# Two attention loops on one core: the logits of two pairs ahead are issued behind the transposes of the current pair

## The reference

```python
# first layer, per block of 128 queries; k_sel, v_sel are the selected keys and values
logits = jnp.einsum('bqgrd,bqkgd->bqgrk', qg, k_sel).astype(jnp.float32) * (ATT_HEAD_DIM ** -0.5)
logits = jnp.where(valid[:, :, None, None, :], logits, -jnp.inf)
p = jax.nn.softmax(logits, axis=-1).astype(dt)
o = jnp.einsum('bqgrk,bqkgd->bqgrd', p, v_sel)
# third layer, block-causal mask
s = (jnp.einsum('bqhd,bkhd->bhqk', qn_b, k_nope)
     + jnp.einsum('bqhr,bkr->bhqk', qp_b, k_pe)).astype(jnp.float32) * scale
s = jnp.where(mask[None, None], s, -jnp.inf)
p = jax.nn.softmax(s, axis=-1).astype(v.dtype)
o = jnp.einsum('bhqk,bkhd->bqhd', p, v)
```

## Time and profile before

| | us |
|---|---|
| runs, median of 3 | 1187.79 |
| runs, lowest and highest | 1187.22, 1194.19 |
| the profiled execution, its own time | 1192.98 |
| its span in the trace | 1190.9 |
| PE busy | 1102.4 (93%) |
| PE weight loads busy | 959.4 (81%) |
| DVE busy | 461.9 (39%) |
| ACT busy | 553.6 (46%) |
| POOL busy | 818.3 (69%) |
| mean granted clock of PE | 0.972 of full |

### The profile page before, as it was taken

How to read it: one execution, slowest core, us unless ns; L and a number is a source line. 1 busy time by engine, 2 the same in 40 slices (tenths; PEclk the granted TensorE clock), 3 DMA queues, 4 the chain that set the end, 5 groups by cost and what they waited for, 6 DMA issues and landing times.

```text
span 1190.9 us, 15744 instructions
## 1 busy us (share of the span) xinstructions
PE 1102.4 (93%) x6630; PEld 959.4 (81%) x6630; DVE 461.9 (39%) x825; ACT 553.6 (46%) x745; POOL 818.3 (69%) x297
## 2 busy tenths in 40 slices
PE   7989999999999655999999989999887998999997
PEld 7877788888899644778888879999886896788886
DVE  4673311159508899531110051711255535111102
ACT  5682544443455564354444344455633534544430
POOL 5703699789498566359979839796575273898880
PEclk9999999999999876999999999999998999999999
DMA  8203655554565300275555435554344144755540
GB/s 347 102 7 120 234 177 179 192 192 146 177 227 191 112 1 1 108 252 189 177 182 189 159 141 213 177 177 147 122 154 143 37 142 159 243 181 178 182 170 36
DMA packets 27445, 186.45 MB, mean 157 GB/s; under 512 B 3168, under 2 KB 3424, under 8 KB 5872
## 3 DMA queue, kind: packets, MB, share of 16 engines
q1 hardware_dynamic: 25184, 178.83, 43.2%
q10 hardware_dynamic: 2192, 6.62, 1.8%
HBM read 184.39 MB, written 1.05 MB: 156 GB/s over the span
## 4 chain that ended last, share of the span: by engine, by line
PE 81%; DVE 12%; POOL 3%; ACT 3%; issue 1%; DMA 1%; DVEq 0%; SPq 0%; ACTq 0%
PE ps L369 25%; PE ps L371 24%; PE ps L370 24%; POOL wl L353 3%; DVE arena L1545 2%; DVE arena L1546 1%; PE ps L1209 1%; PE ps L1939 1%; ACT wh L349 1%; DVE arena L1560 1%; DMA stage<-in_tiles 1%; PE ps L1074 1%; DVE arena L836 1%; DVE arena L814 1%; DVE arena L1554 1%
## 5 line engine op out<-in xcount | busy, mean ns | idle before, releaser
L353 POOL TENSOR_TENSOR wl<-stage,wh 128x2048 fp32r<-128x2048 f32 x166 | 764.6, 4630 | 295.8 <-ACT wh L349 263.9
L349 ACT ACTIVATE wh<-stage 128x2048 fp32r<-128x2048 f32 (+1 forms) x168 | 318.5, 1906 | 89.7 <-DMA stage<-in_tiles 89.1
L369 PE MATMUL ps<-wh,xh 128*128 128x512 f32 (+2 forms) x776 | 293.4, 378 | 20.3 <-POOL wl L353 7.0
L371 PE MATMUL ps<-wh,xl 128*128 128x512 f32 (+2 forms) x776 | 287.9, 371 | 0.0
L370 PE MATMUL ps<-wl,xh 128*128 128x512 f32 (+2 forms) x776 | 287.5, 370 | 0.0
L369 PE MATMUL ps<-xh,wh 128*128 128x256 f32 x644 | 184.1, 286 | 8.5 <-DVE xl L2009 4.1
L369 PEld LDWEIGHTS ps<-wh,xh 128*128 128x128 f32 x776 | 146.8, 189 | 49.7 <-POOL wl L353 5.7
L370 PE MATMUL ps<-xl,wh 128*128 128x256 f32 x644 | 182.7, 284 | 0.0
L371 PE MATMUL ps<-xh,wl 128*128 128x256 f32 x644 | 182.7, 284 | 0.0
L371 PEld LDWEIGHTS ps<-wh,xl 128*128 128x128 f32 x776 | 146.6, 189 | 25.6
L370 PEld LDWEIGHTS ps<-wl,xh 128*128 128x128 f32 x776 | 146.9, 189 | 24.1 <-issue 0.5
(11 more groups left out here) (347 smaller groups left out, 1130.3 us busy)
## 6 DMA issues: line engine op xcount, KB each, us to landing
stage<-in_tiles SPq DMA_DIRECT2D x167, 1024.0 KB, 4.9
arena<-in_ln_g ACTq DMA_DIRECT2D x4, 512.0 KB, 3.5
arena<-in_ln_b ACTq DMA_DIRECT2D x4, 512.0 KB, 5.1
arena<-in_x_t SPq DMA_DIRECT2D x1, 1024.0 KB, 5.3
x_res<-in_x SPq DMA_DIRECT2D x1, 1024.0 KB, 20.5
out<-x_res SPq DMA_DIRECT2D x4, 256.0 KB, 2.2
stage<-in_tiles SPq DMA_DIRECT2D x1, 544.0 KB, 7.4
arena<-in_pre_mix_norm ACTq DMA_DIRECT2D x1, 512.0 KB, 7.0
```

What stands on the lines that cost most here:

```text
L349: nc.scalar.activation(wh[:, ring(n), part], stage[:, ring(n), part], ACT.Copy).then_inc(hi_done, 1)
L353: nc.gpsimd.tensor_tensor(wl[:, ring(n), :], stage[:, ring(n), :], wh[:, ring(n), :].bitcast(F32), ALU.subtract).then_inc(lo_done, 1)
L369: mm(out_, lh, rh, start=start, stop=False, skip_group_check=skip)
L371: return mm(out_, ll, rh, start=False, stop=stop, skip_group_check=skip)
```

## The change

In attend_pe, the block that waits for lg_free and issues logits(i + 2) moves from ahead of the wait for pn_ready(i) to behind the transposes of pair i. PE's turn is then transposes(i), logits(i + 2), value(i - 1). Both attention loops use the function. ACT's and DVE's lists stay as they are, and no buffer or size changes.

```diff
             for i in range(2):
                 logits(i).then_inc(lg_ps.sem, lg_ps.up())
             for i in range(pairs):
-                if i + 2 < pairs:
-                    pe.wait_ge(lg_free.sem, lg_free.due(pe))
-                    logits(i + 2).then_inc(lg_ps.sem, lg_ps.up())
                 pe.wait_ge(pn_ready.sem, pn_ready.due(pe))
                 if i >= 1:
 
...
                         last = nc.tensor.transpose(ps[:, 4 + e, c * P:(c + 1) * P],
                                                    lg[i % 3][:, e, c * P:(c + 1) * P], ident[:])
                 last.then_inc(pt_ps.sem, pt_ps.up())
+                if i + 2 < pairs:
+                    pe.wait_ge(lg_free.sem, lg_free.due(pe))
+                    logits(i + 2).then_inc(lg_ps.sem, lg_ps.up())
                 if i >= 1:
                     value(i - 1)
```

## The result

| | before, us | changed, us |
|---|---|---|
| median | 1190.99 (4 runs) | 1222.54 (4 runs) |
| lowest, highest | 1187.22, 1197.57 | 1220.60, 1224.74 |
| profiled execution, its span | 1190.9 | 1218.6 |
| first loop: first L814 to the first product behind the loop | 32.76 | 54.10 |
| second loop, measured the same way | 23.06 | 34.06 |

The ratio is 1.0259, with a 95% interval of 1.0203 to 1.0315: slower. The two medians differ by 31.6 us. In the two profiled executions the loops lost 21.3 and 11.0 us, and 4.65 us came back between them, in a stretch whose program the change does not touch (last experiments). "First product behind the loop" is the matmul at L369 that starts the next block of weight products.

The account below looks back on a forecast made before the run. DVE was taken to bound the first loop and PE's logits the second. The loops' added 19.0 + 11.6 = 30.6 us, from serial waits and half clock, gave 1218.4 us from a median of 1187.79; range 1208 to 1226.

Parts of the forecast that it names:

- What bounds the loops: Before the change, DVE paces the first loop at 3.57 us a pair; in the second DVE waits for PE's logits.
- The ring: Both loops: normalised(i), transposes(i), logits(i + 2), masked(i + 2), normalised(i + 1) run serially; 5.80 and 8.44 us, adding 13.4 and 8.4.
- transposes until the next group's weight loads: Ring term on PE in both loops: time from the transposes' start to the logits' weight loads, 0.80 us.
- The clock: PE's pauses in both loops halve its granted clock, adding 2 x 1.29 + 2 x 1.5 and 2 x 1.6 us.
- I count two of the four at 1.5 each: First loop's four further pairs, with 2.3 us of PE pause: two assumed at half clock, 1.5 us each.
- the tail: End of the first loop, pairs 6 and 7, with no logits left to issue: forecast unchanged.
- One to one behind the loops: Behind the loops: all work is tied to their end, so their delay passes on whole, none absorbed.
- That the clock stays up: Rival, both loops: the pauses leave PE's clock up, giving 1209.6 us; chance 0.19.
- That every pair falls: Rival, both loops: every pair falls to half clock, giving 1224.0 us; chance 0.24.
- PE did not take the logits past the waiting transposes: Denies a rival on PE's order: logits taken while transposes wait, leaving 1187.8 us; chance 0.02.
- the other side: Rival, not slower: second loop's transposes no longer stand behind logits, saving 0.8 us, giving 1187.0 us; chance 0.01.
- The sum by long pauses alone: Both loops' added time if only the four PE pauses longer than 2.90 us halve the clock: 27.6 us, or 1215.4.

Follow-up runs that it names:

- last experiments: Kernel before and changed kernel, each with an added POOL wait that keeps its L353 off DVE's L2037 and L2039; 1187.96 and 1220.37 us.
- e3: Changed kernel's order within a turn, but with logits issued three pairs ahead instead of two; 1194.15 us, ratio 1.0002 to the kernel before.
- e9: Changed kernel plus a POOL wait until DVE has rotated the queries ahead of the second loop; 1220.37 us, ratio 1.022 to the kernel before.
- e10: Changed kernel with e9's POOL wait and unused matmuls filling PE's pauses in both loops; 1207.89 us, ratio 1.0117 to the kernel before.
- e1: Kernel before with the new order in the first attention loop only; 1215.12 us, ratio 1.016.
- e2: Kernel before with the new order in the second attention loop only; 1209.38 us, ratio 1.011.
- e7: Kernel before plus a POOL wait until DVE has rotated the queries ahead of the second loop; 1186.99 us, ratio 0.9944.
- e8: Kernel before, unchanged, run once more; 1194.92 us in one run.
- e12: Kernel before with e7's POOL wait, run again on the chip of e9 and e10; 1187.96 us, ratio 0.9939 to the kernel before.

## Why the prediction was right

The forecast was 1218.4 us in a range of 1208 to 1226, from a difference of 30.6 us on a median of 1187.8. The measured median is 1222.5, the difference 31.6, with the median of before at 1191.0 once a further run joined it. That the two differences agree within 1 us is partly luck: the ratio's interval leaves 24 to 38 us. The loops themselves lost 32.3 us in the profiles.

- **What bounds the loops** held: DVE sets the pace of the first, PE of the second.
- **The ring** held, and e3 shows it is the mechanism: the same order without the ring costs nothing. Its length was 5.61 us, not 5.80, and 8.23, not 8.44. The term too large was "transposes until the next group's weight loads", 0.80, taken from a row in which values follow transposes. With logits behind them the loads come 0.60 to 0.61 us after the transposes start (85.10 - 84.50 in e3). So the first ring came to 12.3 us instead of 13.4, the second to 30.77 - 23.06 = 7.7 instead of 8.4.
- **The clock** was too small for the first loop: 5.6 us forecast, 9.05 measured (54.10 - 45.05). The step that erred is "I count two of the four at 1.5 each": pairs 2, 3 and 4 all ran slow, with 7.17, 7.27 and 7.07 us a pair against 5.61, pair 5 did not (5.62). The first two long pauses cost 1.05 and 1.92, not 1.29 twice, and the tail, which the forecast left unchanged, lost the remaining 1.4 (clock 0.52 from 112.0 to 115.3 us; transposes(7) lasted 1.40 us). In the second loop 3.2 was forecast and 34.05 - 30.77 = 3.3 measured, though not as forecast: one ring was slow by 1.67 us (9.90 against 8.23), the other kept its 8.23, and the rest fell behind them.
- **The errors cancelled in part:** the rings 1.8 us less, the clock 3.5 more. This, too, is luck.
- **One to one behind the loops** held: e9 shows 32.4 us of the 32.8. The profiled executions alone would have hidden this, as they differ by 27.7: the missing 4.65 us are the collision, there in the profile of before and not in that of the changed kernel, and no part of the forecast. It is also why transposes(2) of the second loop started at 964.87 and not near 969; transposes(6) of the first started at 111.17, with 110 forecast.
- **The rivals.** That the clock stays up is out for the changed kernel; e10 makes that case by hand and comes to 19.9 us. That every pair falls is nearer: five of six pairs of the first loop, one of two of the second, and in e1's first loop and e2's second all of them. PE did not take the logits past the waiting transposes. Of the other side nothing was seen.

The Trainium skill's page "TensorE: Matmul & The Clock Gate", section "Why this matters for your kernels", was cited for the warning that pauses between bursts of matmuls cost the clock. The runs agree, with 9.05 us got back by filling them. The sum by long pauses alone (27.6 us) was too low, since the clock also fell behind pauses of 2.1 to 2.4 us.

## What to carry to other kernels

Before moving work on one engine behind a wait, read the program of the engine that the wait hangs on: if its next instruction needs the moved work, every step between becomes serial, though no instruction was added and each engine has its idle time to spare. The depth counts, not the order: the same order with one more pair ahead was free. A ring that makes TensorE pause costs a second time through its clock, here 12.5 us beside 19.9, and by an amount that differs between runs.

## What the runs showed of the hardware

- Two DVE instructions with SBUF operands stood still while POOL's L353 ran: L2037, two SBUF inputs, 4.67 us instead of 0.69, and L2039, a copy of two columns, 4.34 instead of 0.17. L2035 just ahead of them, with one input in PSUM, kept its 0.69 us (896.13 to 896.82) though L353 had begun at 896.36. The profile books this as busy time of DVE, not as a wait, so the views of waits don't name POOL. The Trainium skill's page "SBUF — State Buffer", section "Who interferes with whom", says that a DVE instruction with two SBUF inputs contends with a GpSimd instruction that reads SBUF, and that one in a two-port mode and GpSimd block each other for the whole instruction. The row of L2037 agrees with the first; that L2039 is in such a mode, no run here shows.
- The granted clock after a pause is not settled by the pause's length. In the changed kernel's first loop the pauses ahead of transposes(2) to (6) were 2.14, 2.29, 2.35, 2.35 and 2.35 us; the clock went to 0.50 in the work behind four of them and stayed at 1.00 behind that of transposes(5). The same pause of 2.9 us lowered it in the profiles of before, e7 and e8 and not in e12's. With the pauses filled it was 1.00 from 66 to 110 us.
